# A two-layer network on one core: the first expert unit's projection in pieces, five rows added by VectorE, block transposes on VectorE, bias rows moved

## The chip, the cores and the metric

The kernel runs on one core of one Trainium2 chip. Its time is the device time of one execution in microseconds; the number to move is the median of the runs. The engines are TensorE (PE, with its weight loads as PEld), VectorE (DVE), ScalarE (ACT), GpSimd (POOL) and SyncE (SP), each with its own queue of instructions; SP and POOL also issue the DMAs. Everything is in 32-bit floats.

## The reference, cut to what matters

There are 512 tokens (256 context, 256 latent) of width 1024 and two layers. Layer 0 mixes them with two recurrences, then passes all 512 through a mixture of experts; layer 1 uses attention and a mixture of experts over the 256 latent tokens. Three places matter here.

```
# modulation rows, one per segment (context, latent), each of 6 * 1024
m = silu(c) @ w_mod[layer] + b_mod[layer]

# gated recurrence, forward and reversed
h_t = a_t * h_(t-1) + u_t

# the other recurrence, per head, forward and reversed
sa    = state @ kk_t
state = state * w_t - sa (x) akk_t + v_t (x) k_t
out_t = state @ r_t

# output projection, then experts: 8 heads, 16 rows of two tables each
x   = x + m[2] * (y @ w_out);  h = modulate(x, m[3], m[4])
act = gelu(u_tab[eidx] . h)
f   = sum over 8 heads and 16 rows of g * act * v_tab[eidx]
```

## The kernel before, in words

Each stage is a block of five instruction queues, joined by semaphores; between two blocks stands a barrier. A wait in a queue holds back all that stands behind it. `step(...)` (class Chain) lets an engine wait for its own last instruction.

**The gated stage** is `rglru` (L512 to L693). It runs over eight units u (two directions by four blocks of 128 channels). TensorE makes the gate matmuls of unit u (L576), ScalarE two tanh (L599) and then three exponentials or tanh (L615 to L617), VectorE `gated` (L646, L648), `vv` (L683) and `scan` (L655 to L666, which needs the roots of L623 from ScalarE). Beside this, eight parts of the modulation rows are made: `mod_groups(n)` on TensorE (L280) multiplies a part of 2 MB of weights that SP loads, `copy_part(n)` on ScalarE (L606) takes it from PSUM, `add_groups(n)` on TensorE (L558) sums the four groups, and `mod_row(n)` on VectorE (L673) adds the bias row. GpSimd stores the row and loads the bias four parts on. TensorE's order is gates of u, part u-1, sum u-3. The sum n needs row n-2, since two banks take turns. VectorE does `mod_row(u - 4)` at the end of units 4 to 7, then scans 5, 6, 7 with rows 4, 5, 6 behind them, then row 7. ScalarE copies part u-1 ahead of the roots of unit u. At its end TensorE has eight matmuls without use (`keep_busy`).

**The scan** is `rwkv_scan`, over eight units of one direction and 128 tokens each. A unit inverts, for each of eight heads, a triangular 128x128 matrix by doubling blocks: T is the inverse as far as blocks of 2^lv. For each level lv from 1 to 6, in two groups g of four heads, the work is

```
X  = NE^T T      (TensorE L883, copied from PSUM by ScalarE L997)
TT = T^T         (TensorE L886, copied from PSUM by ScalarE L1004)
T  = TT^T X where the level's mask says so (TensorE L900, VectorE L1135)
```

TensorE's order in a level is X and TT of group 0, X and TT of group 1, then the last product of both. Level 6 works on halves and ends differently (L880, L902, L1137). Ahead of level 1 stand the masks of four NE and four BF products (L1097) and the first level's masked copy for each group (L1115), all on VectorE. In level 1 TensorE also makes the BV matmuls (L891) and the next unit's `lora` (L789); ahead of group 1 it makes the next unit's `sums` in level 3 (L797) and its `turn` in levels 4 to 6 (L804, L815). GpSimd's `prepare` makes the operands that `turn` reads (L1026 to L1057).

**The experts** are `out_and_experts`, called for layer 0 with four tiles of 128 tokens and for layer 1 with two. `project(i)` (L1592) is the output projection of tile i, `out(i)` and `norm(i)` on VectorE (L1743 to L1755) take it from there, `turn(i)` transposes it (L1606). For each tile and head there is a unit of 16 rows: per row one indirect DMA by GpSimd (L1443) into a ring of eight slots (128 tokens by 8 KB), a dot product on VectorE (L1782), a gelu on ScalarE (L1473, L1531), a diagonal matrix on VectorE (`make_diag`, L1726) and two products on TensorE that add the row into PSUM (L1581; L1652 in the first unit). Between the dots VectorE routes the next unit (`route_part`). In the units of layer 0's first tile, rows 7 and 15 are not multiplied on TensorE but added by VectorE into `pooled` (L1719, L1720). TensorE also makes query products for units to come (L1556, eight parts of them in the first unit, four to a half) and scores (L1564), which ScalarE copies (L1455, L1460). In the first unit TensorE's order is rows 0 to 3, `project(3)`, `turn(2)`, rows 4 and 5, `turn(3)`, then a query part ahead of each row from 6 to 13, a score ahead of rows 10 and 14. ScalarE's copy of the second query half stands ahead of the gelu of row 14.

Of the kernel before, what the change touches and what calls it, by code (L numbers as in the profile page):

```python
# [14 lines left out]
ALU = mybir.AluOpType  # L15
# [486 lines left out]
def rglru(nc, a, xb, gateF, yT, mod, scol, sel, wmod, wmod_in, rows, row_out, gw, gcol, gate_in):  # L502


    with Phase(nc) as ph:
# [23 lines left out]
        with nc.Block() as block:  # L529
# [56 lines left out]
            def _(act):  # L586
# [22 lines left out]
                for u in range(8):  # L609
# [8 lines left out]
                    if u >= 1:  # L618
                        copy_part(u - 1)
                    if u in ROOTS_AT:  # L620
                        act.wait_ge(v_done, u + 1)
                        for q in ROOTS_AT[u]:
                            nc.scalar.activation(vv[:, q], vv[:, q], ACT.Sqrt).then_inc(m_done, 1)  # L623
                copy_part(7)

            @block.vector
            def _(dve):
# [49 lines left out]
                for u in range(8):  # L677
                    if u < 7:
                        gated(u + 1)
                    b = u % 2  # L680
# [5 lines left out]
                    if u >= 4:  # L686
                        mod_row(u - 4)
                for u in range(5, 8):
                    scan(u)
                    mod_row(u - 1)  # L690
                mod_row(7)


def rwkv_scan(nc, a, ident, low, rkv, kk, O, KT, rows_out):
# [13 lines left out]
    with Phase(nc) as ph:  # L708
# [42 lines left out]
         tr_mm, tr_done, pool_own, dve_own, ae_mm, bf_mm, seen_done, bv_mm, bv_done, init_done, x_mm, x_done, tt_mm, tt_done, y_mm, y_done,  # L751
# [3 lines left out]
            "init_done", "x_mm", "x_done", "tt_mm", "tt_done", "y_mm", "y_done", "wu_mm", "wu_low", "wu_high", "r_mm", "r_done", "g_mm",  # L755
# [15 lines left out]
        with nc.Block() as block:  # L771
# [10 lines left out]
            def _(pe):  # L782
# [57 lines left out]
                for n, (d, t) in enumerate(UNITS):  # L840
# [26 lines left out]
                    for lv in range(1, LEVELS):  # L867
                        for g in range(2):
# [16 lines left out]
                            for h in range(4 * g, 4 * g + 4):  # L885
                                m = nc.tensor.transpose(ps[:, 4 + g, (h % 4) * P:(h % 4) * P + P], T[:, h], ident[:])  # L886
                            m.then_inc(tt_mm, 1)
# [5 lines left out]
                        for g in range(2):  # L893
# [3 lines left out]
                            pe.wait_ge(tt_done, 2 * ((LEVELS - 1) * n + lv - 1) + g + 1)  # L897
# [46 lines left out]
            def _(act):  # L944
# [42 lines left out]
                for n, (d, t) in enumerate(UNITS):  # L987
                    for lv in range(1, LEVELS):
                        for g in range(2):
# [9 lines left out]
                            else:  # L999
# [3 lines left out]
                            act.wait_ge(tt_mm, 2 * ((LEVELS - 1) * n + lv - 1) + g + 1)  # L1003
                            nc.scalar.activation(TT[:, 4 * g:4 * g + 4], ps[:, 4 + g].rearrange("p (h t) -> p h t", h=4),  # L1004
                                                 ACT.Copy).then_inc(tt_done, 1)
# [70 lines left out]
            def _(dve):  # L1076
# [32 lines left out]
                for n, (d, t) in enumerate(UNITS):  # L1109
# [7 lines left out]

                    if n == 0:
                        masked_ne(0, 0)
                        masked_ne(0, 1)  # L1120
# [3 lines left out]
                    first_level(0)  # L1124
                    masked_bf(n, 0)
                    first_level(1)
                    for i in range(1, 4):
# [1160 lines left out]
```

## Time and profile before

| | |
|---|---|
| median of 3 runs | 3132.97 us (3131.22 to 3135.37) |
| the profiled execution: its time | 3135.57 us |
| the profiled execution: its span | 3133.7 us |
| mean TensorE clock granted | 0.965 of full |
| TensorE, VectorE, GpSimd, ScalarE busy | 84%, 67%, 35%, 22% |
| moved by DMA | 926.73 MB, 296 GB/s over the span |

The span is what the profile covers; the execution's own time is 1.9 us longer. All times in the trace are microseconds from the start of the span. The stages that the change touches lie at 215 to 297 (gated), 297 to 733 (scan) and 770 to 900 (projection and first expert unit of layer 0).

### The profile page before, as it was taken

The page shows a single profiled execution, that of the slowest core. Times are in us where ns is not written, and L with a number is a line of the kernel's source. Part 1 is how long each engine was busy: PE and PEld are TensorE (multiplying, and loading weights), DVE is VectorE, ACT ScalarE, POOL GpSimd, SP SyncE. Part 2 cuts the span into 40 slices and gives each one's busy share as a digit, 9 for nine tenths or more (in the row PEclk, how much of TensorE's full clock was granted, in tenths as well). Part 3 has the DMA queues.
Part 4 walks back from the last instruction along what each step waited for, and adds up shares of the span by engine and source line. Part 5 has one row for each costly group of instructions (what it writes and reads, how often), then busy time and mean ns, then how long its engine had stood idle before and what let it go on. Part 6 is the DMA issues. An engine that isn't in the chain of part 4 may idle for free. (4 is left out here: it accounts for less than half of the span.)

```text
span 3133.7 us, 31150 instructions
## 1 busy us (share of the span) xinstructions
PE 2625.1 (84%) x9200; PEld 1304.6 (42%) x9200; DVE 2109.5 (67%) x4879; ACT 676.8 (22%) x1701; POOL 1084.4 (35%) x927
## 2 busy tenths in 40 slices
PE   6996999997989998777777777777988788887777
PEld 2441888884444443222222222223434444432222
DVE  2335434345668888888888888886576677778887
ACT  2134343332211111111111111111015211111111
POOL 0002232322134544444444444442000343444443
PEclk9998999999999999999999999999999999999999
DMA  5233000004689999999999999998432799999998
GB/s 192 80 150 136 1 1 1 1 1 175 235 336 407 409 415 410 420 420 421 412 420 420 421 412 419 420 419 328 180 104 100 294 419 420 420 414 419 420 421 331
DMA packets 137679, 926.73 MB, mean 296 GB/s; under 512 B 17488, under 2 KB 18512, under 8 KB 32104
## 3 DMA queue, kind: packets, MB, share of 16 engines
q0 software_dynamic: 113664, 822.20, 63.9%
q1 hardware_dynamic: 23920, 103.31, 8.7%
q8 instruction: 54, 0.88, 0.1%
q14 instruction: 41, 0.34, 0.0%
HBM read 924.33 MB, written 1.11 MB: 295 GB/s over the span
## 5 line engine op out<-in xcount | busy, mean ns | idle before, releaser
L1581 PE MATMUL psum<-ring,diag 128*128 128x512 f32 x2888 | 1406.5, 622 | 345.1 <-DVE diag L1726 344.0
L1443 POOL DMA_INDIRECT ring<-in_uv,experts x768 | 923.3, 1202 | 1243.4 <-PE psum L1581 934.5
L1782 DVE CUSTOM_DVE_ANT_0 ring<-ring,hcur 128x1024 f32<-128x1024 f32 x768 | 941.1, 1225 | 284.8 <-DMA ring<-in_uv,experts 258.2
L1581 PEld LDWEIGHTS psum<-ring,diag 128*128 128x128 f32 x2888 | 523.8, 194 | 1152.0 <-DVE diag L1726 703.8
L1473 ACT ACTIVATE gel<-dots 128x1 f32<-128x1 f32 x736 | 142.7, 201 | 1381.6 <-DVE dots L1782 1380.6
L1726 DVE TENSOR_SCALAR diag<-ident,gel,wcur 128x128 f32<-128x128 f32 x752 | 252.4, 345 | 34.5 <-ACT gel L1531 17.5
L1135 DVE COPY_PREDICATED T<-level,psum 128x512 f32<-128x512 uint32 x80 | 58.6, 733 | 173.8 <-PE psum L900 173.8
L418 PE MATMUL psum<-zT,win_ring 128*128 128x512 f32 x368 | 160.7, 597 | 5.2 <-PEq L90 5.2
L1852 PE MATMUL psum<-wqkv_ring,zT 128*128 128x512 f32 x320 | 137.6, 592 | 2.9 <-PEq L90 2.9
L1556 PE MATMUL psum<-yT,w_q 128*128 128x512 f32 (+1 forms) x256 | 121.1, 579 | 2.9 <-issue 2.9
L418 PEld LDWEIGHTS psum<-zT,win_ring 128*128 128x128 f32 x368 | 70.0, 192 | 90.8 <-issue 90.8
L1852 PEld LDWEIGHTS psum<-wqkv_ring,zT 128*128 128x128 f32 x320 | 60.7, 190 | 79.1 <-issue 79.1
L997 ACT ACTIVATE X<-psum 128x512 f32<-128x512 f32 x80 | 47.8, 597 | 183.8 <-PE psum L883 183.0
L883 PE MATMUL psum<-T,NE 128*128 128x128 f32 x640 | 86.0, 277 | 0.0
L900 PE MATMUL psum<-X,TT 128*128 128x128 f32 x640 | 85.1, 279 | 0.0
L541 POOL DMA_DIRECT2D yT<-in_b_mod x16 | 8.0, 506 | 214.6 <-POOLq L90 214.6
L900 PEld LDWEIGHTS psum<-X,TT 128*128 128x128 f32 x640 | 78.1, 191 | 6.5 <-issue 3.3
L883 PEld LDWEIGHTS psum<-T,NE 128*128 128x128 f32 x640 | 78.2, 191 | 6.1 <-issue 3.3
L1556 PEld LDWEIGHTS psum<-yT,w_q 128*128 128x128 f32 x256 | 49.6, 196 | 61.7 <-issue 59.6
L1652 PE MATMUL psum<-ring,diag 128*128 128x512 f32 x120 | 60.2, 633 | 13.4 <-DVE diag L1726 13.4
L1671 DVE MAX8 val<-sc 128x8 f32<-128x128 f32 x200 | 57.9, 290 | 18.6 <-ACT sc L1511 15.1
L1556 PEld LDWEIGHTS psum<-oT,w_q 128*128 128x128 f32 x256 | 48.1, 193 | 47.0 <-issue 45.6
(401 smaller groups left out, 2785.6 us busy)
## 6 DMA issues: line engine op xcount, KB each, us to landing
wmod<-in_w_mod SPq DMA_DIRECT2D x32, 1024.0 KB, 8.6
w_q<-in_w_q SPq DMA_DIRECT2D x36, 512.0 KB, 8.1
wmod<-in_w_mod POOLq DMA_DIRECT2D x16, 1024.0 KB, 5.6
ring<-in_uv,experts POOLq DMA_INDIRECT x768, 10.8
wqkv_ring<-in_w_qkv SPq DMA_DIRECT2D x6, 2048.0 KB, 9.6
win_ring<-in_w_in SPq DMA_DIRECT2D x23, 512.0 KB, 3.7
w_all<-in_w_o SPq DMA_DIRECT2D x8, 512.0 KB, 7.5
scores<-in_w_out SPq DMA_DIRECT2D x6, 512.0 KB, 5.7
```

Source lines behind the costliest of these rows:

```text
L418: m = nc.tensor.matmul(ps[:, c % BANKS], wring[:, c % RING, k], zT[:, k], start=(k == 0), stop=(k == KD - 1))
L883: m = nc.tensor.matmul(ps[:, g, (h % 4) * P:(h % 4) * P + P], NE[:, h, 0], T[:, h], start=True, stop=True)
L900: m = nc.tensor.matmul(ps[:, 2 + g, (h % 4) * P:(h % 4) * P + P], TT[:, h], X[:, h], start=True, stop=True)
L1135: nc.vector.copy_predicated(T[:, hs], mask, ps[:, 2 + g].rearrange("p (h t) -> p h t", h=4)).then_inc(y_done, 1)
L1443: nc.gpsimd.indirect_dma_start(ring[:, s % RING], None, uv, bass.IndirectOffsetOnAxis(ap=experts[:, n, j:j + 1], axis=0)).then_inc(row_in[ ...
L1473: nc.scalar.activation(gel[:, j:j + 1], dots[:, j:j + 1], ACT.Gelu_apprx_tanh).then_inc(gelu_done, 1)
L1556: i = nc.tensor.matmul(q_bank(m)[:, cols], w_q[:, m, k], hT[:, k, cols], start=(k == 0), stop=(k == KD - 1))
L1581: m = nc.tensor.matmul(ps[:, c], diag[:, j % DIAGS], ring[:, j % RING, D + 512 * c:D + 512 * c + 512], start=(first and j == 0), stop=(las ...
L1652: m = nc.tensor.matmul(ps[:, c], diag[:, j % DIAGS], ring[:, j % RING, D + 512 * c:D + 512 * c + 512], start=(j == 0), stop=False, skip_gr ...
L1726: nc.vector.tensor_scalar(diag[:, j % DIAGS], ident[:], gel[:, j:j + 1], wcur[:, j:j + 1], ALU.mult, ALU.mult).then_inc(diag_done, 2 if po ...
L1782: nc.vector.tensor_tensor_reduce(u, u, hcur[:], 1.0, 0.0, ALU.mult, ALU.add, dots[:, j:j + 1]).then_inc(dot_done, 1)
L1852: m = nc.tensor.matmul(ps[:, i % 8], zT[:, k, t * P:(t + 1) * P], wring[:, c % RING, k], start=(k == 0), stop=(k == KD - 1))
```

## The change

It does three things.

1. In `rglru` VectorE does `mod_row(u - 3)` in units 3 to 7, ahead of `vv` and the scans, and in the tail row u ahead of scan u. ScalarE's `copy_part(6)` moves behind the roots of unit 7.
2. In `rwkv_scan` the transposed T of levels 1 to 5, whose blocks are at most 32 wide, is made by VectorE's transpose (`turn_blocks`), which turns each 32x32 block where it stands, straight from T into TT. Level 6 keeps TensorE's transposes and ScalarE's copy. The transposes of a level stand on VectorE's queue right behind the masked copy of the level before.
3. In `out_and_experts`, in the first unit of layer 0, `project(3)` is cut into four pieces of two weight slices, one ahead of each of rows 1, 2, 3 and 4; and rows 7, 9, 11, 13 and 15 are added by VectorE instead of 7 and 15. GpSimd's loads into their slots wait for the added row. Other units keep rows 7 and 15; layer 1 has no such rows.

```
# rglru, ScalarE
-                    if u >= 1:
+                    if 1 <= u < 7:
                         copy_part(u - 1)
...
+                copy_part(6)
                 copy_part(7)
# rglru, VectorE
                 for u in range(8):
                     if u < 7:
                         gated(u + 1)
+                    if u >= 3:
+                        mod_row(u - 3)
                     b = u % 2
...
                     for q in SCAN_AT.get(u, ()):
                         scan(q)
-                    if u >= 4:
-                        mod_row(u - 4)
                 for u in range(5, 8):
+                    mod_row(u)
                     scan(u)
-                    mod_row(u - 1)
-                mod_row(7)
# rwkv_scan, TensorE
-                            for h in range(4 * g, 4 * g + 4):
-                                m = nc.tensor.transpose(ps[:, 4 + g, (h % 4) * P:(h % 4) * P + P], T[:, h], ident[:])
-                            m.then_inc(tt_mm, 1)
+                            if lv == LEVELS - 1:
+                                for h in range(4 * g, 4 * g + 4):
+                                    m = nc.tensor.transpose(ps[:, 4 + g, (h % 4) * P:(h % 4) * P + P], T[:, h], ident[:])
+                                m.then_inc(tt_mm, 1)
...
-                            pe.wait_ge(tt_done, 2 * ((LEVELS - 1) * n + lv - 1) + g + 1)
+                            if lv < LEVELS - 1:
+                                pe.wait_ge(tv_done, 2 * ((LEVELS - 2) * n + lv - 1) + g + 1)
+                            else:
+                                pe.wait_ge(tt_done, 2 * n + g + 1)
# rwkv_scan, ScalarE
-                            act.wait_ge(tt_mm, 2 * ((LEVELS - 1) * n + lv - 1) + g + 1)
-                            nc.scalar.activation(TT[:, 4 * g:4 * g + 4], ps[:, 4 + g].rearrange("p (h t) -> p h t", h=4),
-                                                 ACT.Copy).then_inc(tt_done, 1)
+                            if lv == LEVELS - 1:
+                                act.wait_ge(tt_mm, 2 * n + g + 1)
+                                nc.scalar.activation(TT[:, 4 * g:4 * g + 4], ps[:, 4 + g].rearrange("p (h t) -> p h t", h=4),
+                                                     ACT.Copy).then_inc(tt_done, 1)
# rwkv_scan, VectorE
+                    def turn_blocks(lv, g):
+                        dve.wait_ge(y_done, 2 * (LEVELS * n + lv - 1) + g + 1)
+                        hs = slice(4 * g, 4 * g + 4)
+                        nc.vector.transpose(TT[:, hs].rearrange("p h t -> p (h t)"),
+                                            T[:, hs].rearrange("p h t -> p (h t)")).then_inc(tv_done, 1)
...
                     first_level(0)
+                    turn_blocks(1, 0)
                     masked_bf(n, 0)
                     first_level(1)
+                    turn_blocks(1, 1)
                     for i in range(1, 4):
                         masked_bf(n, i)
...
                                 nc.vector.copy_predicated(T[:, hs], mask, ps[:, 2 + g].rearrange("p (h t) -> p h t", h=4)).then_inc(y_done, 1)
+                                if lv + 1 < LEVELS - 1:
+                                    turn_blocks(lv + 1, g)
# out_and_experts
+        FIRST_POOLED = (RING - 1, RING + 1, RING + 3, RING + 5, TOPK - 1) if NT == TILES else ()
+        def pooled_at(n, j):
+            return j in FIRST_POOLED if isinstance(n, int) and n == 0 else POOLED(j)
+        def pooled_count(n, j):
+            if isinstance(n, int) and n == 0:
+                return FIRST_POOLED.index(j) + 1
+            return n * (TOPK // RING) + len(FIRST_POOLED) - TOPK // RING + j // RING + 1
...
-                        if RING <= s < HEADS * TOPK + RING and POOLED(j):
-                            pool.wait_ge(pooled_done, (s - RING) // RING + 1)
+                        if RING <= s < HEADS * TOPK + RING and pooled_at((s - RING) // TOPK, (s - RING) % TOPK):
+                            pool.wait_ge(pooled_done, pooled_count((s - RING) // TOPK, (s - RING) % TOPK))
...
                 for j in range(TOPK):
+                    if NT > 2 and 1 <= j <= 4:
+                        project(3, 2 * j - 2, 2 * j)
                     if NT > 2 and j == 4:
-                        project(3)
                         turn(2)
...
-                    if POOLED(j):
+                    if pooled_at(0, j):
                         continue
```

`make_diag` and the counts of `mm_done` and `diag_done` use `pooled_at` and `pooled_count` in the same way.

## Rows read from the trace of the kernel before

**Rows 1.** The page: span, busy time by engine, one kind of DMA.
```profile
span 3133.7 us, 31150 instructions
...
PE 2625.1 (84%) x9200; PEld 1304.6 (42%) x9200; DVE 2109.5 (67%) x4879; ACT 676.8 (22%) x1701; POOL 1084.4 (35%) x927
...
wmod<-in_w_mod SPq DMA_DIRECT2D x32, 1024.0 KB, 8.6
```

**Rows 2.** Stretches: length, busy us by engine, TensorE clock, DMA share, GB/s.
```profile
215.00:297.00 82.00, 56.37 (x192) 15.21 (x193) 41.75 (x66) 41.38 (x66) 12.10 (x25) 0.81 0.39 155
297.00:733.00 436.00, 419.03 (x3532) 358.50 (x3532) 167.36 (x266) 155.91 (x293) 121.31 (x107) 0.98 0.02 8
...
900.00:2165.00 1265.00, 1025.93 (x2254) 405.74 (x2253) 1038.68 (x2625) 206.76 (x654) 600.94 (x491) 0.98 1.00 413
```

**Rows 3.** Timeline of TensorE, gated stage: start, us, instructions, [idle before, releaser].
```profile
247.64 1.87 PE L558 MATMUL psum<-acc,sel 128*2 128x512 f32 x2 [6.45 <-DVE yT L673]
...
287.81 8.34 PE L291 MATMUL psum<-xb,gw 128*128 128x512 f32 x16
297.01 3.24 PE L291 MATMUL psum<-kk,ident 128*128 128x512 f32 x7 [0.85 <-PEq L90]
```

**Rows 4.** Timeline of VectorE, gated stage.
```profile
246.81 0.68 DVE L673 SCALAR_TENSOR_TENSOR yT<-psum,yT 2x512 f32<-2x512 f32 x1
...
270.12 0.69 DVE L683 SCALAR_TENSOR_TENSOR vv<-tn 128x512 f32<-128x512 f32 x1
...
289.60 1.28 DVE L673 SCALAR_TENSOR_TENSOR yT<-psum,yT 2x512 f32<-2x512 f32 x2
```

**Rows 5.** Timeline of ScalarE, gated stage.
```profile
244.09 0.59 ACT L606 ACTIVATE acc<-psum 128x512 f32<-128x512 f32 x1
...
253.08 1.26 ACT L599 ACTIVATE th<-psum,gcol 128x512 f32<-128x512 f32 x2 [8.40 <-PE psum L576]
...
263.96 1.27 ACT L599 ACTIVATE th<-psum,gcol 128x512 f32<-128x512 f32 x2 [3.81 <-PE psum L576]
```

**Rows 6.** Timeline of all engines, scan, level 2 of a unit.
```profile
490.12 0.97 PEld L883 LDWEIGHTS psum<-T,NE 128*128 128x128 f32 x8
...
491.01 0.47 PEld L886 LDWEIGHTS psum<-ident,T 128*128 128x128 f32 x4
...
491.32 0.60 ACT L997 ACTIVATE X<-psum 128x512 f32<-128x512 f32 x1 [1.19 <-PE psum L883]
...
492.78 2.04 PEld L900 LDWEIGHTS psum<-X,TT 128*128 128x128 f32 x16
...
493.98 0.73 DVE L1135 COPY_PREDICATED T<-level,psum 128x512 f32<-128x512 uint32 x1 [2.82 <-PE psum L900]
...
494.77 0.97 PEld L883 LDWEIGHTS psum<-T,NE 128*128 128x128 f32 x8
```

**Rows 7.** Groups by line, VectorE: busy us, mean ns, idle before.
```profile
L1135 DVE COPY_PREDICATED T<-level,psum 128x512 f32<-128x512 uint32 x80 | 58.6, 733 | 173.8 <-PE psum L900 173.8
...
L1154 DVE TENSOR_TENSOR low<-low,ident 128x512 f32<-128x512 f32 x8 | 5.5, 692 | 0.3
...
L646 DVE TENSOR_SCALAR la<-th,sp_b 128x512 f32<-128x512 f32 x8 | 3.9, 486 | 27.5 <-ACT th L599 27.5
```

**Rows 8.** Timeline of VectorE where GpSimd works beside it.
```profile
311.68 1.70 DVE L1087 TENSOR_TENSOR t<-t,rkv 128x512 f32<-128x512 f32 x1
```

**Rows 9.** Timelines of VectorE and TensorE, first expert unit.
```profile
856.10 1.29 DVE L1743 TENSOR_TENSOR h<-psum,gate 128x512 f32<-128x512 f32 x2 [1.41 <-PE psum L1592]
...
889.61 1.88 PE L1652 MATMUL psum<-ring,diag 128*128 128x512 f32 x4
891.33 1.88 PE L1556 MATMUL psum<-yT,w_q 128*128 128x512 f32 x4
...
897.46 0.35 DVE L1726 TENSOR_SCALAR diag<-ident,gel,wcur 128x128 f32<-128x128 f32 x1 [8.61 <-issue]
...
899.60 0.40 DVE L1773 COPY wcur<-weights 128x16 f32 x1 [0.41 <-DVE pooled L1720]
```

More of the change, by code:

```diff
@@ L750, in rwkv_scan @@
         (up_in, c_in, lr0_zero, lr1_zero, state_zero, pre_done, lora_mm, lora_th, lw_done, na_done, sums_mm, exp_done, ends_mm, ends_done, q_done, rb_done, bn_done, kb_done, qb_done,
-         tr_mm, tr_done, pool_own, dve_own, ae_mm, bf_mm, seen_done, bv_mm, bv_done, init_done, x_mm, x_done, tt_mm, tt_done, y_mm, y_done,
+         tr_mm, tr_done, pool_own, dve_own, ae_mm, bf_mm, seen_done, bv_mm, bv_done, init_done, x_mm, x_done, tt_mm, tt_done, tv_done, y_mm, y_done,
          wu_mm, wu_low, wu_high, r_mm, r_done, g_mm, g_done, s0_done, s_mm, s_done, o_mm, o_done) = ph.sems(
@@ L754, in rwkv_scan @@
             "bn_done", "kb_done", "qb_done", "tr_mm", "tr_done", "rwkv_pool", "rwkv_dve", "ae_mm", "bf_mm", "seen_done", "bv_mm", "bv_done",
-            "init_done", "x_mm", "x_done", "tt_mm", "tt_done", "y_mm", "y_done", "wu_mm", "wu_low", "wu_high", "r_mm", "r_done", "g_mm",
+            "init_done", "x_mm", "x_done", "tt_mm", "tt_done", "tv_done", "y_mm", "y_done", "wu_mm", "wu_low", "wu_high", "r_mm", "r_done", "g_mm",
             "g_done", "s0_done", "s_mm", "s_done", "o_mm", "o_done")
@@ L1653, in _ @@
                                              start=(j == 0), stop=False, skip_group_check=True)
-                    m.then_inc(mm_done, 2 if POOLED(j + 1) else 1)
+                    m.then_inc(mm_done, 2 if pooled_at(0, j + 1) else 1)
                 with pe.Fori(1, HEADS - AHEAD) as hd:
@@ L1716, in make_diag @@
                 def make_diag(n, j, step, pooled_tile):
-                    if pooled_tile and POOLED(j):
+                    if pooled_tile and pooled_at(n, j):
                         dve.wait_ge(gelu_done, n * TOPK + j + 1)
@@ L1721, in make_diag @@
                                                        ALU.mult, ALU.add).then_inc(pooled_done, 1)
-                        dve.wait_ge(pooled_done, n * (TOPK // RING) + j // RING + 1)
+                        dve.wait_ge(pooled_done, pooled_count(n, j))
                         return
@@ L1726, in make_diag @@
                     nc.vector.tensor_scalar(diag[:, j % DIAGS], ident[:], gel[:, j:j + 1], wcur[:, j:j + 1],
-                                            ALU.mult, ALU.mult).then_inc(diag_done, 2 if pooled_tile and POOLED(j + 1) else 1)
+                                            ALU.mult, ALU.mult).then_inc(diag_done, 2 if pooled_tile and pooled_at(n, j + 1) else 1)
                 nc.vector.memset(scores[:, NU], 0.0).then_inc(pad_done, 1)
```

## The prediction

> **What bounds the kernel now.** I read the page's header and busy shares first [rows 1]: TensorE is busy 2625 of 3133.7 us, but that is an average over stages with different limits. So I then cut the span into stages [rows 2]. In the gated stage (215 to 297) no engine is busy for more than 56.4 of 82 us: it is bound by waits. In the scan (297 to 733) TensorE is busy 419 of 436 us and no other engine over 40%: TensorE's work sets the time. From 900 to 2165 the expert rows' DMA share is 1.00 at 413 GB/s, so a microsecond gained ahead of that stage is kept only if the stream of rows starts a microsecond earlier. The change touches one thing in each of the first two stages and the first expert unit of layer 0, which lies ahead of that stream.
>
> In the gated stage the timeline of TensorE shows its waits [rows 3]: 6.45 us for VectorE's bias row L673 before the sum matmul at 247.64. VectorE's own timeline [rows 4] gives that row at 246.81, behind a scan that nothing on TensorE wants. ScalarE's [rows 5] shows the price: it sits 8.40 us idle before the gates at 253.08 and 3.81 us before those at 263.96, both for gate matmuls that stand behind such a sum on TensorE's queue.
>
> In the scan I read one ordinary inner level [rows 6]. Starts of weight loads give TensorE's queue: X group 0 at 490.12, its transposes at 491.01, Y at 492.78, next level at 494.77: a level of 4.65 us, with 0.89 us for four products and 0.44 for four transposes (0.47 by duration). The level's closing masked copy starts at 493.98, lasts 0.73 and ends 0.06 before the next level's products. So both TensorE's queue (4.45 us of work) and the dependent chain nearly fill the level.
>
> **Part 1, the bias rows.** mod_row(n) moves one unit earlier on VectorE, ahead of the unit's vv and scan; copy_part(6) moves behind the last roots. Row 0 now stands at about 235.6, where its sum has long been made, and costs its 0.68 us [rows 4] there; roots wait for a table load at that place, which hides it. The sum at 247.64 is then not late. ScalarE is free for the next gates when its copy at 244.09 ends, 244.7 [rows 5], instead of 253.08: 8.4 us. The gates at 263.96 lose their idle 3.8 as well, since the row they hung on (row 1) now comes ahead of a scan. What follows on both engines moves 12.2 us: VectorE's last vv from 270.12 to 257.9, say 258.1 with a row ahead of it. Before, VectorE worked without a gap from 270.12 to 290.88 (289.60 + 1.28) [rows 4], 20.8 us with five rows in it; two of these now lie ahead of vv, 1.4 us, so it ends at 258.1 + 19.4 = 277.5. TensorE ends later than VectorE before: eight warming matmuls take 8.34 us from 287.81, to 296.15, and the next stage starts 0.86 later at 297.01 [rows 3]. They stand behind the last sum, which waits for row 5. Row 5 now goes ahead of scan 5, at about 264.5, so TensorE is through at 265.2 + 1.9 + 8.3 = 275.4, inside VectorE's time. The row's own waits are short: row 0's sum stands on TensorE's queue ahead of unit 4's gates, and its bias was asked for at the stage's start; GpSimd's stores of the rows and loads of the next biases hang on the rows and start earlier with them. Behind the moved copy_part(6) stands only the sum of part 6, for row 6 at about 269, eight microseconds later. The stage ends at 277.5 + 0.9 = 278.4 instead of 297.0: **18.5 us**. What could be late next are the modulation weights: 8.6 us from issue to landing [rows 1]; the last two are asked for when part 5 is multiplied, about 246.6, are there at 255.3, and their sum is wanted at 264.5. Bounds: 12.2 if the tail is not shortened, 18.5 as worked out. I take 18.5, since each term is a row.
>
> **Part 2, the block transposes.** TensorE loses, per unit, transposes of levels 1 to 5: 10 groups of 0.44 us, 4.4 us, 35 us over eight units, and ScalarE loses the same number of copies. VectorE gains ten 128x512 transposes per unit, 80 in all, each behind the masked copy of its group. No transpose on VectorE is in the trace. Bounds: 0.49 us, the fastest 128x512 form, and 1.70, a 128x512 operation that met GpSimd [rows 7, 8]. I take 0.70, from the ordinary one-element form at 0.69 [rows 7], the nearest in work. In a run of instructions without a wait the next begins about 0.1 earlier, so it occupies 0.6.
>
> An ordinary level then goes: masked copy 0.73 + 0.05, transpose 0.60, second masked copy 0.73 + 0.06, X group 1 0.89, Y group 0 0.89 with 0.31 until VectorE sees it (1.20 from the load at 492.78 to the copy at 493.98 [rows 6]). Sum 4.26, against 4.65: 0.4 won, not 0.9, since VectorE's transpose now sits between the two copies. Where other work stands ahead of X group 1, it hides that: in level 3 the sums of the next unit, in levels 4 and 5 its operand turns. Following one unit through: level 1 loses 0.7, because its two transposes stand ahead of three masked BF products which the BV matmuls want; level 2 wins that 0.7 back; level 3 wins 0.9, level 4 0.8, level 5 0.8. So a unit gains 2.5. GpSimd's preparation of the next unit starts 0.7 later and its second operand arrives just as TensorE asks for it: it is the next limit. Seven such units are 17.5; the last has no next unit to hide behind and gains 1.2. Together **18.7 us**. At 1.25 us for a transpose the same walk gives level 1 another 1.1 and level 5 another 0.55: about 0.85 a unit, less than 0 in the last, 4.5 us in all.
>
> The Trainium skill, "VectorE: DVE Perf Modes", section "The three transpose paths", gives 311 ns for 128x128 in bf16 on VectorE, in 32x32 blocks only. Taken four times for four heads it would be an estimate of 1.24 us and the change's sum 28 instead of 42; taken as a fixed part and one element per cycle it is close to the 0.70. No row before shows which.
>
> **Part 3, the first expert unit.** project(3) is cut in four, between rows 0 to 3; rows 9, 11 and 13 leave TensorE and go with 7 and 15 to VectorE. Before, the output of tile 3 (L1743) waits 1.41 us for the projection at 856.10 [rows 9]. A row takes TensorE 1.72 us (889.61 to 891.33 [rows 9]). project(3) is 32 such passes, four to a row's 1.72, so 8 x 1.72 = 13.7 us in all. TensorE stands idle between rows 0 to 3 before, for their diagonals; a piece of 3.4 us between two rows covers that. The same work without the idle ends about 1.4 earlier, and so does all that hangs on L1743. I take the whole 1.4. Later the diagonal of row 14 waits at 897.46 for a gel that stands behind the query copy on ScalarE, and that for TensorE's eighth query part [rows 9]. Rows 9 and 11 stood ahead of it: 2 x 1.72 = 3.4 us. So row 14 and the next unit's start, 899.60, move 1.4 + 3.4 = **4.9 us**. VectorE pays about 1.1 more for each of three rows; it is idle 8.61 ahead of 897.46, which hides it. If that cover were gone it would cost 3.4. The change adds a wait on GpSimd's queue: the loads into the slots of rows 9, 11 and 13 now wait for VectorE's added rows, and every later load stands behind them. By the same order they are added at about 872, 884 and 888, each earlier than TensorE was through with that row, so the row stream moves too. Bound: 1.4 (if the stream does not follow) to 4.9.
>
> **The sum.** 18.5 + 18.7 + 4.9 = 42.1. Against the profiled execution, 3135.57 us, that gives 3093.5; the median of the runs is 2.6 below that execution, so 3091.
>
> **Rivals.** *Slow transposes* (about 1.25 us): for it, an operation not in the trace; against, ordinary forms at 0.69 [rows 7]. Gain 18.5 + 4.5 + 4.9 = 28: 3105. *The shared port*: a VectorE operation with two SBUF inputs met GpSimd at 311.68 and took 1.70 instead of 0.69 [rows 7, 8], and GpSimd works through levels 2 to 5. If transposes met it so, six a unit would hold up GpSimd's operands by 0.5 each, and level 4 would wait: about 1.5 us lost per unit rather than 2.5 won, so +12 on the scan: gain 11, 3122. Against it: the masked copies, with one SBUF input, stay at 0.73 in the same levels [rows 6, 7]. The Trainium skill, "SBUF — State Buffer", section "Who interferes with whom", says that a VectorE instruction with at most one SBUF input, outside the two-port modes, doesn't contend with GpSimd; by that, this rival falls. *VectorE becomes the scan's bound*: a transpose of 2.3 us makes the level 2 x (0.78 + 2.3) = 6.2 and level 1 loses 3.9; a unit loses 4, the scan 32, and the kernel is 9 us slower, 3142. It decides from about 2 us. Three times the ordinary form speaks against it. *Waits only change hands* in the gated stage or the first unit: 12.2 and 1.4 instead of 18.5 and 4.9, so gain 32: 3101.
>
> **How the numbers follow.** The forecast 0.66; waits change hands 0.11; slow transposes 0.12; the port 0.06; VectorE the bound 0.04; 0.01 for the rest. The likeliest one's own range is 3083 to 3098. The range takes in the two next cases up to 3108, and down to 3080 for a transpose at 0.49 and TensorE's whole 35 us coming through in part. A measurement of this kernel can't tell under 0.2%, 6.3 us, from no change. Faster by more 0.94, within it 0.02, slower 0.04.
>
> **What would show it.** A stage start at 278 to 279 instead of 297.0, and no idle over 2 us of TensorE for L673. 80 VectorE transposes of 0.7 us in the scan, a level of 4.3 instead of 4.65 us, the scan's stretch shorter by 17 to 20. The copy of weights that opens the second unit at about 858 (899.6 less 42), and the expert stage after it unchanged in length. It would be wrong if transposes last over 1 us, if GpSimd's operations grow, or if the row stream keeps its old start.

## The result, and the profile after

The changed kernel takes 3094.07 us (3091.99 to 3098.07, 4 runs) against 3133.74 (3131.22 to 3135.37, 4 runs) on the same chip: 39.7 us less, ratio 0.9876 with a 95% interval of 0.9859 to 0.9893. The forecast was 3091.0, range 3080 to 3108. The profiled execution of after took 3091.99 us.

The page of after begins so (span, then busy time by engine), and answers to [rows 1]:

```profile
span 3090.2 us, 30503 instructions
...
PE 2584.4 (84%) x8868; PEld 1266.2 (41%) x8868; DVE 2166.5 (70%) x4962; ACT 637.9 (21%) x1621; POOL 1085.1 (35%) x927
```

TensorE gave up 40.7 us of work and VectorE took on 57.0, yet the span is 43.5 shorter: busy time by itself does not give the gain. The same stretches as in [rows 2], cut at the same places of the program (first bias load, first load of the scan, end of the scan; then from the expert stage's first load to the second expert unit, and the stream of rows). After the length stand the busy us of TensorE, its weight loads, VectorE, ScalarE and GpSimd, the share of the full clock that TensorE was granted, the DMA share and GB/s:

```profile
214.00:276.00 62.00, 48.68 (x192) 13.33 (x192) 41.95 (x67) 41.01 (x66) 12.03 (x24) 0.92 0.51 205
276.00:694.00 418.00, 389.83 (x3217) 325.27 (x3218) 221.84 (x348) 117.96 (x214) 121.30 (x107) 0.99 0.02 8
730.00:856.00 126.00, 111.02 (x344) 57.91 (x345) 70.44 (x155) 26.85 (x57) 24.12 (x23) 0.93 0.71 272
856.00:2121.00 1265.00, 1028.69 (x2249) 407.17 (x2248) 1038.05 (x2624) 206.86 (x654) 606.05 (x490) 0.97 1.00 413
```

Measured from mark to mark, the gated stage went from 81.9 to 62.0 us (19.9 won), the scan from 436.5 to 417.7 (18.8), the stretch from the expert stage's first load to the copy that opens the second unit from 128.8 to 124.9 (3.9). That is 42.6. Where the code is the same, another 0.9 lies ahead of the gated stage and 0.9 between the scan and the expert stage, so that the second unit starts 44.5 us earlier (855.13 instead of 899.60); from there to the end of the kernel 1.0 is given back. From the second unit to the end of the tile nothing changed length (302.1 in both), and the stream of rows runs at the same 413 GB/s with a share of 1.00. So what was won ahead of the stream was kept to within 1 us.

1.7 us of the gated stage's 19.9 are luck of the two profiled executions. The change's profile is granted the full clock through the stage's first 40 us and has VectorE's third `vv` (L686) 14.8 us after the stage's first instruction; before has it at 16.5, with a granted clock below full in the first 4 us. The other twelve profiles of this study fall on these two values too, whichever version of the stage they hold: eight have 16.5, four have 14.8.

**The gated stage after**: first VectorE's bias rows, then TensorE, ScalarE and VectorE at the points that [rows 3 to 5] show for before (start, us, instructions, idle ahead and its releaser):

```profile
240.93 0.68 DVE L674 SCALAR_TENSOR_TENSOR yT<-psum,yT 2x512 f32<-2x512 f32 x1
...
241.22 0.59 ACT L606 ACTIVATE acc<-psum 128x512 f32<-128x512 f32 x1
...
241.74 1.27 ACT L599 ACTIVATE th<-psum,gcol 128x512 f32<-128x512 f32 x2
...
255.73 0.69 DVE L686 SCALAR_TENSOR_TENSOR vv<-tn 128x512 f32<-128x512 f32 x1
...
262.83 1.86 PE L558 MATMUL psum<-acc,sel 128*2 128x512 f32 x2 [3.22 <-DVE yT L674]
...
264.63 9.20 PE L291 MATMUL psum<-xb,gw 128*128 128x512 f32 x16
...
276.26 4.53 PE L291 MATMUL psum<-kk,ident 128*128 128x512 f32 x10 [2.44 <-PEq L90]
```

The reader is to see that the gates follow the copy at 241.22 at once, where [rows 5] had 8.40 us of idle (`th` is their output); that the last vv is at 255.73; and that TensorE's last wait for a bias row is 3.22 us, now in front of work that ends at 273.8, before VectorE's last instruction (274.48 plus 0.69) does. The stage ends by VectorE's own work.

**The scan after**, levels 1 and 2 of the fourth unit, all engines; it answers to [rows 6]:

```profile
452.59 0.72 DVE L1120 COPY_PREDICATED T<-level,psum 128x512 f32<-128x512 uint32 x1
...
453.34 0.71 DVE L1126 STREAM_TRANSPOSE TT<-T 128x512 f32<-128x512 f32 x1
...
453.98 0.65 DVE L1102 TENSOR_TENSOR BF<-psum,seen 128x512 f32<-128x512 f32 x1
...
456.74 1.13 PE L883 MATMUL psum<-T,NE 128*128 128x128 f32 x8 [0.83 <-DVE BF L1102]
...
463.13 2.06 PEld L883 LDWEIGHTS psum<-T,NE 128*128 128x128 f32 x16
...
465.11 1.93 PEld L904 LDWEIGHTS psum<-X,TT 128*128 128x128 f32 x16
...
466.31 0.74 DVE L1148 COPY_PREDICATED T<-level,psum 128x512 f32<-128x512 uint32 x1 [1.40 <-PE psum L904]
...
467.08 0.71 DVE L1126 STREAM_TRANSPOSE TT<-T 128x512 f32<-128x512 f32 x1
467.10 0.97 PEld L883 LDWEIGHTS psum<-T,NE 128*128 128x128 f32 x8
467.10 1.16 PE L883 MATMUL psum<-T,NE 128*128 128x128 f32 x8
```

A transpose takes 0.71 us, and the next instruction begins 0.64 after its start. TensorE's loads run X, Y, X without transposes between them, and level 2 lasts 3.97 us from load to load. The price stands at 456.74: X of the second four heads waits 0.83 for a mask that stood behind a transpose. VectorE's groups over the scan (busy us, mean ns, idle ahead), which answer to [rows 7]:

```profile
L1148 DVE COPY_PREDICATED T<-level,psum 128x512 f32<-128x512 uint32 x80 | 57.7, 721 | 99.7 <-PE psum L904 99.7
L1126 DVE STREAM_TRANSPOSE TT<-T 128x512 f32<-128x512 f32 x80 | 56.9, 712 | 2.8
```

Distances from the unit's first masked copy to X of each level, from TensorE's starts, in the unit shown in [rows 6] and in the one above (us):

| | before | after | won | forecast |
|---|---|---|---|---|
| first copy to X of level 1 | 1.99 | 2.19 | -0.2 | } -0.7 |
| level 1 | 8.06 | 8.46 | -0.4 | } |
| level 2 | 4.62 | 3.86 | 0.76 | 0.7 |
| level 3 | 6.36 | 5.50 | 0.86 | 0.9 |
| level 4 | 6.36 | 5.59 | 0.77 | 0.8 |
| level 5, to the next masked copy | 4.22 | 3.46 | 0.76 | 0.8 |

The whole unit (from the first copy of one to that of the next, mean of seven) went from 51.8 to 49.3. The unit shown takes 48.9; four of the seven take 49.6, since TensorE waits there in level 4 for an operand that GpSimd makes for the next unit:

```profile
376.46 0.63 PE L815 MATMUL psum<-ident,rb 128*128 128x128 f32 x4 [0.60 <-POOL rb L1059]
```

Before, no unit has this wait. It is the "next limit" of the forecast, and it is reached in four units. In the last unit, which has no next unit's work to hide behind, a level went from 4.65 to 4.24 us, where the forecast had 4.26.

**The first expert unit after**, VectorE; it answers to [rows 9]:

```profile
815.03 1.28 DVE L1768 TENSOR_TENSOR h<-psum,gate 128x512 f32<-128x512 f32 x2
...
841.68 0.48 DVE L1751 TENSOR_SCALAR diag<-ident,gel,wcur 128x128 f32<-128x128 f32 x1 [8.36 <-ACT gel L1555]
...
852.98 0.35 DVE L1751 TENSOR_SCALAR diag<-ident,gel,wcur 128x128 f32<-128x128 f32 x1 [4.36 <-ACT gel L1555]
...
855.13 0.18 DVE L1798 COPY wcur<-weights 128x16 f32 x1 [0.41 <-DVE pooled L1745]
```

The wait of 1.41 us ahead of the fourth tile's output is gone. From that output to the last diagonal it is 37.95 us, before 41.36: 3.4 less, two rows of TensorE. The last wait on gel is 4.36 instead of 8.61.

### The profile page after: what moved, and what is told of

It reads as the page before. It is cut to its first block and busy times, and to the rows that moved or that the text cites. A ratio compares the mean times of both kernels' runs of the same rounds, so it can differ in the third digit from the quotient of the medians.

```text
span 3090.2 us, 30503 instructions
## 1 busy us (share of the span) xinstructions
PE 2584.4 (84%) x8868; PEld 1266.2 (41%) x8868; DVE 2166.5 (70%) x4962; ACT 637.9 (21%) x1621; POOL 1085.1 (35%) x927
## 5 line engine op out<-in xcount | busy, mean ns | idle before, releaser
L1605 PE MATMUL psum<-ring,diag 128*128 128x512 f32 x2888 | 1407.6, 623 | 344.5 <-DVE diag L1751 342.5
L1148 DVE COPY_PREDICATED T<-level,psum 128x512 f32<-128x512 uint32 x80 | 57.7, 721 | 99.7 <-PE psum L904 99.7
L1696 DVE MAX8 val<-sc 128x8 f32<-128x128 f32 x200 | 57.9, 289 | 18.6 <-ACT sc L1535 15.1
L1887 POOL DMA_DIRECT2D wmod<-in_w_mod x16 | 8.6, 535 | 165.7 <-DVE mod_acc L1917 131.9
```

The costliest lines, as they stand in the source:

```text
L1605: m = nc.tensor.matmul(ps[:, c], diag[:, j % DIAGS], ring[:, j % RING, D + 512 * c:D + 512 * c + 512], start=(first and j == 0), stop=(las ...
L1696: step(nc.vector.max(values[:, lo:lo + 8], src))
```

## Experiments

Each version was timed four to twelve times beside the kernel before. The median of the kernel before differed by up to 2 us between these sets of runs (3133.05, 3135.03 and 3135.05), so where versions of different sets are compared with each other, their ratios count.

**The three parts alone.** The diff in three: the bias rows with the copy's move (*rows_only*); the transposes (*turns_only*); the first expert unit (*experts_only*).

```
rows_only     + if u >= 3:  mod_row(u - 3)        # ahead of vv and scan
              + for u in range(5, 8): mod_row(u); scan(u)
              + copy_part(6) behind the last roots
turns_only    + turn_blocks(lv, g) on VectorE for levels 1 to 5, none on TensorE and ScalarE
experts_only  + FIRST_POOLED, project(3, 2 * j - 2, 2 * j) between rows
```

> Part 1 alone on the kernel before. The theory that the three parts add gives its own term, 18.5 us faster. If waits only change hands in the gated stage, 12.2. If the gain of this part is in truth another part's, under 10.

> Part 2 alone on the kernel before. The walk through one unit gives 18.7 us faster. If all of TensorE's freed work came through it would be 35; if VectorE's added 57 us were in the way it would be near 0.

> Part 3 alone on the kernel before. 4.9 us faster if the row stream follows the earlier start of the second unit; 1.4 or less if the later stream, full with DMA, takes it back.

Measured: *rows_only* 3115.55 (before 3133.05), ratio 0.9940 [0.9926, 0.9954]: 17.5 us. *turns_only* 3117.77, 0.9948 [0.9934, 0.9962]: 15.3, and 16.3 by the ratio. *experts_only* 3129.57, 0.9991 [0.9982, 1.0000]: 3.5, and 2.8 by the ratio. Together 36 to 38 of the 39.7: the parts add up, within what these intervals allow. Each part won in its own stage: in the profile of *rows_only* the gated stage is 64.3 us long, in that of *turns_only* 82.6 and the scan 422.4. That scan is 14.1 shorter than before's, against 18.8 in the full change. The clock accounts for the difference. The first four units take the same time in both traces (48.9 to 49.6 us); the next three take 50.5, 51.2 and 51.1 instead of 48.9, 49.6 and 49.6, which is 4.8 us. In each of these three TensorE drops to the lower of its two levels in the unit's last third; the first one's row, and the same row of the change one unit earlier:

```profile
557.03 3.51 PE L912 MATMUL psum<-qb,TT 128*128 128x128 f32 x16 [0.51 <-DVE TT L1152]
...
487.33 2.05 PE L912 MATMUL psum<-qb,TT 128*128 128x128 f32 x16 [0.52 <-DVE TT L1152]
```

The waits ahead are the same, so the trace doesn't say why the clock fell in one and not in the other. Single units of other traces show it as well, one in before; each such unit is about 1.6 us longer. In the gated stage of *rows_only* the profile has the 16.5 us of before ahead of the third `vv`, so its 17.6 us won compares like with like.

**The bias rows without the copy's move.** *rows_only* with `copy_part(u - 1)` for u of 1 to 7 as before:

```
-                    if 1 <= u < 7:
+                    if u >= 1:
                         copy_part(u - 1)
```

> The kernel before with the moved bias rows (VectorE's half in units 3 to 7 instead of behind them) but ScalarE's copy of part 6 left where it was. The rows alone with the move of that copy won 17.5 us. If the copy's move is worth nothing, as I costed it, the same: 3115 to 3116, ratio 0.994. Rival: the copy of part 6 (of 8.4 us waits) holds ScalarE's gates of the last unit back, and its move is 2 us or more of the gain: 3118 or more.

Measured 3117.84 (before 3135.05), ratio 0.9946 [0.9931, 0.9960]: 17.2 us, beside 17.5 of *rows_only* by the medians; 17 and 19 by the ratios, whose intervals overlap widely. The stage is 63.9 us long, beside 64.3. So the move of the copy is worth nothing that these runs show, as it was costed.

**What stood at the stage's end before.** The kernel before without the eight warming matmuls (16 passes) behind the last sum; they compute nothing that is used:

```
-                keep_busy(nc, ps[:, 0], gw[:, 0], xb[:, 0], 8)
```

> The kernel before without the eight warming matmuls at the end of the gated stage. If they set the stage's end, 5.3 us faster, as VectorE ends at 290.9 and TensorE at 296.2. If something else holds the barrier, or the scan pays it back with a colder TensorE, no difference.

Measured 3130.0 (before 3135.03), ratio 0.9987 [0.9978, 0.9996]: 4.1 us by the ratio (1.3 to 6.9), 5.0 by the medians. The stage ends at 292.5 instead of 297.0; 1.7 of that is again the early part of the stage, since this profile has the third `vv` at 14.8 us. From the last `vv` to TensorE's first matmul of the scan it is 26.9 us before, 24.5 without the warming matmuls and 20.5 in the change. So the warming matmuls were on the path in the kernel before, but by 2.4 us of this trace, not by the 5.3 that TensorE ended later than VectorE [rows 3, 4]. Without them VectorE is through at 288.85 and the scan starts 3.7 us later:

```profile
287.57 1.28 DVE L672 SCALAR_TENSOR_TENSOR yT<-psum,yT 2x512 f32<-2x512 f32 x2
...
288.55 1.10 POOL L548 DMA_DIRECT2D modulation_rows<-yT  x2 [3.90 <-DVE yT L672]
...
292.52 0.95 POOL L1059 MEMSET lr<- 128x1024 f32 x1 [2.87 <-POOLq L90]
```

GpSimd's store of the last row begins only after that row is made. That it holds the stage's end is argued from these rows, not shown by a run. In the change the last row is made at 270.81, and neither the store nor the matmuls end behind VectorE. Of the 6.4 us by which the tail got shorter (26.9 to 20.5), 1.4 are the two rows that now lie ahead of the last `vv`; the other 5.0 is what stood between VectorE's last instruction and the scan, 6.1 us before and 1.1 in the change.

**How much a transpose costs.** The changed kernel with every VectorE transpose done twice, 80 more in all (`flat` is the view of four heads as 128x512):

```
+                        step(nc.vector.transpose(flat(TT), flat(T)))
                         nc.vector.transpose(flat(TT), flat(T)).then_inc(tv_done, 1)
```

> The changed kernel with every VectorE transpose done twice, 0.75 us more each, 60 us in all on VectorE. The walk says that levels 3 and 4 hide it behind the next unit's work and levels 1 and 5 pay 2.3 us a unit: 17 us slower than the changed kernel. If VectorE's queue were the scan's bound, 60 slower; if TensorE alone were, no slower.

Measured 3133.55 (3117 to 3141; before 3135.03), ratio 0.9988 [0.9974, 1.0002]: 35 us more than the change by the ratios, 39 by the medians, where the walk said 17. Level 1 of the fourth unit in its trace:

```profile
468.64 1.13 PE L883 MATMUL psum<-T,NE 128*128 128x128 f32 x8 [0.88 <-DVE BF L1102]
...
471.34 1.13 PE L883 MATMUL psum<-T,NE 128*128 128x128 f32 x8 [1.57 <-DVE BF L1102]
...
472.45 3.45 PE L892 MATMUL psum<-rkv,BF 128*128 128x64 f32 x16
...
475.69 2.02 PE L904 MATMUL psum<-X,TT 128*128 128x128 f32 x8
...
477.50 2.91 PE L789 MATMUL psum<-up,lr 128*128 128x512 f32 x4
```

and the windows of this and the next stretch, with the granted clock as the third column from the end:

```profile
468.00:475.00 7.00, 4.79 (x29) 4.49 (x30) 4.32 (x7) 1.19 (x2) 0.00 (x0) 0.84 0.00 1
475.00:481.00 6.00, 6.00 (x24) 4.46 (x24) 2.15 (x3) 1.75 (x3) 0.00 (x0) 0.62 0.01 3
```

The change has these rows too, shorter:

```profile
457.84 2.00 PE L892 MATMUL psum<-rkv,BF 128*128 128x64 f32 x16
...
459.68 1.11 PE L904 MATMUL psum<-X,TT 128*128 128x128 f32 x8
...
460.62 1.89 PE L789 MATMUL psum<-up,lr 128*128 128x512 f32 x4
```

```profile
454.00:461.00 7.00, 6.05 (x49) 5.15 (x46) 3.93 (x8) 1.79 (x3) 0.00 (x0) 1.00 0.00 0
461.00:467.00 6.00, 6.00 (x44) 5.10 (x42) 3.39 (x5) 2.39 (x4) 3.52 (x4) 1.00 0.01 3
```

TensorE stood idle for 0.88 and 1.57 us within 3 us, and then worked in part at the lower of its two levels (a granted clock of 0.62 over 6 us): 1.45 + 0.91 + 1.02 = 3.4 us more for the same matmuls. The waits themselves cost 1.5 us up to the end of level 1 and 0.7 in level 5, where X of the second group now waits 0.51 for VectorE; levels 3 and 4 hide theirs. That is 5.5 us together, by which this unit (54.4) exceeds the change's (48.9).

The same two waits did not always bring the lower level. The second unit of the same trace has them too, and its BV takes 2.00 us:

```profile
361.74 1.13 PE L883 MATMUL psum<-T,NE 128*128 128x128 f32 x8 [0.87 <-DVE BF L1102]
...
364.45 1.13 PE L883 MATMUL psum<-T,NE 128*128 128x128 f32 x8 [1.58 <-DVE BF L1102]
365.55 2.00 PE L892 MATMUL psum<-rkv,BF 128*128 128x64 f32 x16
```

This unit takes 51.8 us, 2.2 more than the change's second. In five of the eight units the lower level followed in level 1, in three it did not; in none of the change's eight did it. What decides between the five and the three isn't shown.

So the walk was right about the waits: it said 2.3 us a unit, and the trace has about 2.2 in each of the first seven and 4.5 in the last, 20 us in all beside its 17. What it did not hold is the clock. Over the scan TensorE's clock is 0.95, the change's 0.99; in this trace the lower level lasts 38 us longer than in the change's scan, which at half speed is 19 us. Both together are the 39 by which the profiled scan is longer. The runs bear it out: they scatter from 3117 to 3141 us, and the fastest, 23 us above the change, has the highest granted clock of the twelve (0.966; the others 0.955 to 0.961).

**The price of level 1, taken away.** In *behind_masks*, the two transposes of level 1 go behind the three masks:

```
                     first_level(0)
-                    turn_blocks(1, 0)
                     masked_bf(n, 0)
                     first_level(1)
-                    turn_blocks(1, 1)
                     for i in range(1, 4):
                         masked_bf(n, i)
+                    turn_blocks(1, 0)
+                    turn_blocks(1, 1)
```

In *level1_tensor*, level 1's transposes go back to TensorE, and their copies to ScalarE:

```
-                            if lv == LEVELS - 1:
+                            if lv in (1, LEVELS - 1):
                                 for h in range(4 * g, 4 * g + 4):
                                     m = nc.tensor.transpose(...)
```

ScalarE's copies and the counts that the engines wait for are changed to match, and the two `turn_blocks(1, g)` go.

> The changed kernel, with the two transposes of level 1 moved behind the three masked BF products. The walk charges level 1 with 0.7 us a unit for their place and gives back 0.75 of TensorE's freed work as well: 1.4 x 8 = 11 us faster than the changed kernel, 51 faster than before. If the first level isn't where time is lost, no difference from the changed kernel, 40 faster than before.

> The changed kernel with level 1's transposes back on TensorE and ScalarE. The walk says 0.7 us a unit better than the changed kernel, 5.5 us faster than it, and less than with the transposes moved behind the masks. If the place on VectorE costs nothing it is 7 us slower, by TensorE's 0.9 us a unit.

Measured: *behind_masks* 3082.82, ratio 0.9836 [0.9823, 0.9849], 11 to 13 below the change (by the times and by the ratios); *level1_tensor* 3089.98, 0.9854 [0.9840, 0.9868], 4 to 7 below it. In the first, X of both groups runs as one row, with a wait of 0.33 us for its load instead of 0.83 between them:

```profile
455.02 1.86 PEld L883 LDWEIGHTS psum<-T,NE 128*128 128x128 f32 x16 [0.33 <-DVE T L1120]
455.03 2.05 PE L883 MATMUL psum<-T,NE 128*128 128x128 f32 x16
...
456.64 1.29 DVE L1126 STREAM_TRANSPOSE TT<-T 128x512 f32<-128x512 f32 x2
...
456.92 1.90 PE L892 MATMUL psum<-rkv,BF 128*128 128x64 f32 x16
...
458.65 1.11 PE L904 MATMUL psum<-X,TT 128*128 128x128 f32 x8
```

The transposes end at 457.9, before Y wants them at 458.65. A unit takes 48.2 us instead of 49.3.

**The two together.** *behind_masks* with every transpose done twice tells whether VectorE's work or its place costs:

> The kernel with the level-1 transposes behind the three masks, and each of VectorE's 80 transposes done twice (the second one's result is the one used). With the transposes between the masks, doing them twice cost 38 to 40 us, of which the walk had forecast 17. Theory: the doubled transposes hold back the BF masks of level 1, TensorE falls idle there for 0.88 and 1.57 us, and after that its granted clock is 0.72 in the next 12 us (1.00 in the kernel after); in levels 3 and 4 the doubled transposes cost nothing, since X starts at the same distances in both (5.49 and 5.60 us). Behind the masks nothing waits for the first doubled pair until Y: so it should cost 0 to 6 us over the 3083 us of the version behind the masks, say 3086 (ratio 0.985), and the clock stays at 0.98 in the scan. Rival: the doubling costs by its work on VectorE wherever it stands (80 x 0.71 = 57 us, two thirds of it in the open as before): 3120 to 3125, ratio 0.996.

Measured 3092.00 (before 3135.05), ratio 0.9857 [0.9840, 0.9874]: 7 us above *behind_masks* by the ratios, 9 by the medians, at and over the upper end of what the theory gave, 30 below the rival. A unit is 49.1 instead of 48.2. Two of the seven units fall to the lower clock in their last third, one of *behind_masks*; apart from that a unit is about 0.7 longer and the last 3.0, which makes 8. The row that holds the 0.7 is at level 5:

```profile
478.16 0.71 DVE L1127 STREAM_TRANSPOSE TT<-T 128x512 f32<-128x512 f32 x1
478.18 1.16 PE L883 MATMUL psum<-T,NE 128*128 128x128 f32 x8 [0.51 <-DVE T L1149]
```

The same 57 us of added VectorE work cost 35 to 39 between the masks and 7 to 9 behind them. By the traces, the waits were 20 and 8 of that, and the clock is most of the rest: over the scan it is 0.97 here (expected 0.98) instead of 0.95, and no unit falls to the lower level in its level 1.

**VectorE's order in the levels.** *behind_masks*, with both masked copies of a level ahead of both transposes:

```
                                 nc.vector.copy_predicated(T[:, hs], mask, ...).then_inc(y_done, 1)
-                                if lv + 1 < LEVELS - 1:
-                                    turn_blocks(lv + 1, g)
...
+                        if lv + 1 < LEVELS - 1:
+                            turn_blocks(lv + 1, 0)
+                            turn_blocks(lv + 1, 1)
```

> The kernel with the level-1 transposes behind the masks, and in levels 1 to 4 VectorE does both masked copies first and both transposes after them, so that X of the second four heads waits 0.71 us less. Theory A: with the masks out of the way the levels are bound by TensorE, which is busy without a gap from 450 to 480 us in that kernel's trace, so the order makes no difference: 3081 to 3084, ratio 0.983 to 0.984. Theory B: VectorE's chain of copy, transpose, copy still sets the level's period (by my walk 3.85 instead of 4.26 us in levels that hold no other work): 3 to 7 us less, 3076 to 3080.

Measured 3079.89, ratio 0.9831 [0.9817, 0.9845]: the value lies in theory A's range by the ratio and just inside theory B's by the time (3076 to 3080), 1.6 us below *behind_masks* by the ratios, which the intervals don't tell from nothing. The units speak for A: where neither trace has the lower clock they are 0.05 to 0.08 us shorter; only the last one, which has no next unit's work to fill TensorE, is 1.8 shorter (from its first masked copy to the end of the scan 41.1 for 42.9). It has the lowest time of this study, without being told apart from *behind_masks*.

**The first expert unit in its two parts.** Only the fourth tile's projection in pieces, and only the five rows:

```
pieces_only   + if NT > 2 and 1 <= j <= 4:  project(3, 2 * j - 2, 2 * j)
added_only    + FIRST_POOLED and its counts;  project(3) at j == 4 as before
```

> The kernel before with the fourth tile's projection in four pieces, and rows 7 and 15 alone added by VectorE. 1.4 us faster by the term in the sum, which is at the edge of what can be told; the trace should show the output of tile 3 without its wait of 1.4 us and the second unit starting 1.4 earlier.

> The kernel before with the first expert unit's five rows of 16 added by VectorE, and the fourth tile's projection in one piece as before. Both together won 3.5 us (expected 4.9), the pieces alone 1.3 with an interval that holds nothing. By the terms of the forecast the rows alone are worth 3.4: 3130, ratio 0.9989. Rival: the two only work together (the pieces make TensorE late for the rows, or the rows give it back waiting for VectorE), and the rows alone win under 1 us.

Measured: *pieces_only* 3133.28, ratio 0.9996 [0.9988, 1.0005]; *added_only* 3132.65 (before 3135.05), 0.9991 [0.9982, 1.0000], the same as both together. So the rows carry the part. The pieces do remove the wait: their trace has the output without idle,

```profile
856.20 1.28 DVE L1744 TENSOR_TENSOR h<-psum,gate 128x512 f32<-128x512 f32 x2
```

but 85.5 us after the expert stage's first load, and before it was 85.3. VectorE was late already at the first tile's output, which lies ahead of all pieces (20.2 instead of 18.6 us after that load), and it is as late there in *added_only*, which has none (20.3): this moves between executions. From the third tile's output on, the fourth's comes 13.0 us later instead of 14.5, so the wait is won there. From the third tile's output to the start of the second unit it is 56.8 to 58.2 us in five profiles with the stage as before (mean 57.7), 56.9 with the pieces alone, 53.9 with the rows alone and 52.2 to 54.9 in seven with both (mean 53.5). That gives the rows about 3.8 us, both together 4.2, and the pieces 0.8 alone or 0.4 on top of the rows, less than these profiles differ among themselves.

## Why the prediction was right, point by point

- **Bias rows, 18.5 us.** The stage gave 19.9 in the change, 1.7 of it by the clock in the stage's first microseconds, and 17.6 with this part alone; the runs gave 17.5 (19 by the ratio). The gates follow at once at 241.74, as said. The forecast moved the last `vv` by 12.0; measured from the stage's first instruction it moved 13.5, or 11.8 without those 1.7. The tail behind it was forecast 6.6 shorter and is 6.4, but the reason given for it is only in part right: the warming matmuls that the forecast had as the stage's end cost 2.4 us there (*no_warming*), and behind them something else would have held the end, probably the last row's store. One sign of the forecast failed: TensorE was to have no idle over 2 us for a bias row, and has 3.22 at 262.83. It costs nothing, since VectorE ends later. The warming matmuls took 9.20 us in the change, not 8.34, hidden by VectorE's own work.
- **Transposes, 18.7 us.** The scan gave 18.8. The terms of the walk came out within 0.1 us each, the level-1 term at 0.6 for 0.7. The price I took, 0.70, is 0.711 to 0.716 in 80 of 80, so the bound of 0.49 below and of 1.70 above are both out. So is the estimate of 1.24 that could be drawn from the Trainium skill, "VectorE: DVE Perf Modes", section "The three transpose paths". The 0.71 is what the other reading of that figure had; with one shape measured, no run here parts it into a fixed part and one per element.
- **The port rival fell.** Of the 80 transposes 35 overlap a GpSimd operation, and none of these takes over 716 ns; GpSimd's operations are 1.27 us in both traces. The Trainium skill, "SBUF — State Buffer", section "Who interferes with whom", had it so for an instruction with at most one SBUF input outside the two-port modes, and the trace agrees: 0 of 35 slowed, where a two-input operation took 1.70 [rows 8].
- **VectorE as the bound fell too, but the point where transposes turn the gain was put too high.** I wrote that they decide against the change from about 2 us each, and that at 1.25 us the part would still win 4.5. *twice* puts about 1.4 us there (its two transposes start 0.75 apart, and one takes 0.64 to the next instruction), and it lost 35 to 39 us, twice what the transposes had won: the point lies well below 2 us. What the walk left out is the price of a wait besides its length: of the 39 us in the profile the waits are 20, near the walk's 17, and the lower clock behind them is 19. In the change itself the wait is short (0.83), the clock in the scan stays at 0.99, and the forecast held. It held by that: no term of it would have shown that the clock could fall. For transposes of 1.25 us no run was made.
- **First expert unit, 4.9 us.** 3.5 and 2.8 in the runs, 3.9 in the profile, 4.2 over all profiles. The rows' 3.4 is right to a tenth in the trace (41.36 to 37.95). The mis-sized term is the 1.4 for the pieces: the wait of 1.41 goes, but at the second unit 0.4 to 0.8 of it is left, within the spread, and the run can't tell it from nothing.
- **The row stream follows**, as said: the length from the second unit on is 302.1 in both.

## What to carry to other kernels

Where an operation moves to an engine with time to spare, walk its queue instruction by instruction: 57 us of doubled transposes cost 7 to 9 us behind the masks that TensorE waits for and 35 to 39 us in front of them, and moving two of a unit's ten behind the masks won 11 to 13 us over the change. A wait that vanishes from the profile is a gain only as far as what follows it starts earlier. A wait that TensorE has in the middle of dense work can have a second price, which a walk with fixed durations leaves out: compare the granted clock of windows right after it. And before a difference between two profiles is explained by the code, compare the granted clock of the same stretch, unit by unit: here it made 1.6 us in single units and 1.7 us in one stage, between stretches with the same code.

## What was not expected of the hardware

- A transpose of 128x512 in f32 on VectorE takes 711 to 716 ns, against 692 of an ordinary two-input operation and 721 of a masked copy of the same shape. It also did not slow down beside GpSimd, in 35 of 35.
- Two idle spells of TensorE, 0.88 and 1.57 us within 3 us, were followed by a granted clock of 0.84 and 0.62, and BV took 3.45 us instead of 2.00; so in five of eight units of *twice*, and not in the other three with the same spells. With one spell of 0.83 the clock stayed at 1.00 there in all eight units of the change.
- In the kernel before, the warming matmuls did not pay for themselves: 8.34 us of them stood at the end of the stage, and without them it is 4.1 us faster (1.3 to 6.9), and the scan behind them is 1.2 us shorter in its profile, not longer.
